# One table set for logarithm and exponential, shorter warm runs, and a head's mean square from two single-pass products in a two-layer encoder trunk

## The reference, cut to what matters

```python
def rmsnorm(x, g, eps=EPS):
    y = x * rsqrt(mean(x * x) + eps) * g
for layer in range(2):
    sh1, sc1, g1, sh2, sc2, g2 = split(silu(c) @ ada_w[layer] + ada_b[layer], 6)
    h = rmsnorm(x, norm_g[layer, 0]) * (1 + sc1) + sh1
    y = diff_attention(h) if layer == 0 else conformer_conv(h)
    x = x + g1 * y
    h = rmsnorm(x, norm_g[layer, 1]) * (1 + sc2) + sh2
    x = x + g2 * conv_ffn(h)
return rmsnorm(x, final_g)
# in diff_attention, per head: p = softmax(a) - lam * softmax(b); o = p @ v
#   o = rmsnorm(o, subln_g, 1e-5) * (1 - lambda_init), over the 128 values of a head
# in conformer_conv: silu(layernorm(causal_dwconv(glu(h @ w_pw1 + b_pw1), w_dw) + b_dw)) @ w_pw2 + b_pw2
```

## Time and profile before

| | |
|---|---|
| median of 3 runs (lowest to highest) | 1267.98 us (1267.55 to 1268.33) |
| the profiled execution: its time | 1265.96 us |
| the profiled execution: its span | 1264.2 us |
| mean granted clock of the matrix engine | 0.976 of full |
| busy share of the span: PE, DVE, ACT, POOL | 97%, 56%, 45%, 43% |
| chain that ended last, by engine | PE 81%, DVE 12%, issue 3%, ACT 2% |

### The profile page before, as it was taken

How to read it: one execution, slowest core, us unless ns; L and a number is a source line. 1 busy time by engine, 2 the same in 40 slices (tenths; PEclk the granted TensorE clock), 3 DMA queues, 4 the chain that set the end, 5 groups by cost and what they waited for, 6 DMA issues and landing times.

```text
span 1264.2 us, 16847 instructions
## 1 busy us (share of the span) xinstructions
PE 1231.0 (97%) x5494; PEld 983.4 (78%) x5494; DVE 702.3 (56%) x1157; ACT 567.5 (45%) x899; POOL 540.8 (43%) x273
## 2 busy tenths in 40 slices
PE   7999999989999999999999999999999999999996
PEld 7877777667888888888888776577888888888884
DVE  5667766753766733346887899972533333340002
ACT  4366656644543344442223666762544444442221
POOL 1333322223433444444442699744344444454440
PEclk6899999999999999999998999999999999999998
DMA  9744443222456422236763222113233232232321
GB/s 360 214 151 148 146 154 133 101 100 67 149 184 199 166 90 93 92 105 230 232 244 112 83 84 67 33 34 100 67 100 100 100 100 90 93 106 95 105 78 66
DMA packets 45639, 157.04 MB, mean 124 GB/s; under 512 B 5536, under 2 KB 5792, under 8 KB 45600
## 3 DMA queue, kind: packets, MB, share of 16 engines
q1 hardware_dynamic: 44928, 156.21, 37.0%
q10 hardware_dynamic: 672, 0.34, 0.1%
HBM read 154.10 MB, written 2.42 MB: 124 GB/s over the span
## 4 chain that ended last, share of the span: by engine, by line
PE 81%; DVE 12%; issue 3%; ACT 2%; POOL 1%; DMA 1%; DVEq 0%; SPq 0%; ACTq 0%; POOLq 0%
PE psum L917 24%; PE psum L918 24%; PE psum L919 24%; DVE psum L1754 6%; PE psum L947 2%; PE psum L928 1%; DVE psum L1480 1%; DVE pt_lo L1489 1%; PE psum L951 1%; PE psum L1074 1%; DVE acc L1331 1%; DMA ada_first<-ada_w 1%; POOL acc_p L515 1%; PE psum L1101 1%; PE psum L1113 0%
## 5 line engine op out<-in xcount | busy, mean ns | idle before, releaser
L502 POOL TENSOR_TENSOR w_lo<-w_raw,w_hi 128x1024 fp32r<-128x1024 f32 (+1 forms) x192 | 455.2, 2387 | 670.6 <-ACT w_hi L589 670.6
L917 PE MATMUL psum<-h_hi,w_hi 128*128 128x512 f32 x1152 | 465.9, 404 | 4.1 <-DVE x L1584 2.2
L918 PE MATMUL psum<-h_lo,w_hi 128*128 128x512 f32 x1152 | 452.5, 393 | 0.0
L919 PE MATMUL psum<-h_hi,w_lo 128*128 128x512 f32 x1152 | 452.1, 392 | 0.0
L917 PEld LDWEIGHTS psum<-h_hi,w_hi 128*128 128x128 f32 x1152 | 219.0, 190 | 54.3 <-issue 7.2
L919 PEld LDWEIGHTS psum<-h_hi,w_lo 128*128 128x128 f32 x1152 | 218.5, 190 | 46.9
L918 PEld LDWEIGHTS psum<-h_lo,w_hi 128*128 128x128 f32 x1152 | 218.7, 190 | 45.6 <-issue 3.4
L589 ACT ACTIVATE w_hi<-w_raw 128x1024 fp32r<-128x1024 f32 (+1 forms) x192 | 195.6, 1032 | 82.7 <-DMA w_raw<-w_tiles 82.6
L917 PE MATMUL psum<-a_hi,w_hi 128*128 128x512 f32 x352 | 137.1, 390 | 1.0 <-issue 1.0
L919 PE MATMUL psum<-a_hi,w_lo 128*128 128x512 f32 x352 | 137.0, 389 | 0.0
L918 PE MATMUL psum<-a_lo,w_hi 128*128 128x512 f32 x352 | 136.9, 389 | 0.0
(11 more groups left out here) (185 smaller groups left out, 1342.7 us busy)
## 6 DMA issues: line engine op xcount, KB each, us to landing
w_raw<-w_tiles SPq DMA_DIRECT2D x160, 512.0 KB, 3.4
ada_buf<-ada_w SPq DMA_DIRECT2D x32, 512.0 KB, 3.4
w_raw<-w_tiles SPq DMA_DIRECT2D x32, 448.0 KB, 3.2
ada_late<-ada_w SPq DMA_DIRECT2D x28, 512.0 KB, 5.2
ada_mid<-ada_w SPq DMA_DIRECT2D x20, 512.0 KB, 4.5
ada_first<-ada_w SPq DMA_DIRECT2D x16, 512.0 KB, 10.1
x<-x_in SPq DMA_DIRECT2D x4, 512.0 KB, 7.0
bias<-rel_scratch SPq DMA_DIRECT2D x8, 256.0 KB, 6.1
```

What stands on the lines that cost most here:

```text
L502: nc.gpsimd.tensor_tensor(w_lo[:, slot, 0:k], w_raw[:, (ph.tile + l) % 2, 0:k], f(w_hi[:, slot, 0:k]), ALU.subtract).then_inc(lo_done, 1)
L917: nc.tensor.matmul(dst, w_hi[:, slot, k], rhs_hi, start=first, stop=False)
L918: nc.tensor.matmul(dst, w_hi[:, slot, k], rhs_lo, start=False, stop=False)
L919: return nc.tensor.matmul(dst, w_lo[:, slot, k], rhs_hi, start=False, stop=last)
```

## The change

Five things change.

2. **A head's mean square.** ACT squares in place, in bank `OB`, and writes a rounded copy of the squares, `sq_hi`; DVE forms the rest, `sq_lo`, after its last piece of the conditioning and ahead of the bias of that (`ada_out`); PE multiplies both by ones of type fp32r, `ones_r`, which ACT makes once.
3. **Warm runs.** `keep_warm` has 12 repetitions instead of 18 ahead of UP0 and UP1, and 16 instead of 24 ahead of PW2.
4. **The seventh late chunk.** `last_ada(6)` moves from norm 2 to behind the layer norm's sums, ahead of `keep_warm(16)`; its sum lies in `acc_last`, its result in another bank.
5. **`late_out`** is called twice: for six chunks where it was, and for the seventh in the layer norm on DVE, behind the variance (L1778).

```diff
@@ -86,6 +86,7 @@
...
 PW1_FROM_2 = Phase(PW1.group + 2, PW1.tile + 4, 2, DK - 2)
+LN_EXP_SET = 6
 LATE0 = 4 + 8 * HEADS
@@ -165,6 +166,7 @@
...
         ones = sb("ones", [P, P])
+        ones_r = sb("ones_r", [P, P], F32R)
         big = cursor[0]
@@ -205,6 +207,8 @@
...
         o_sq = at("o_sq", [P, S], F32, offset_of["pad_v"])
+        sq_hi = at("sq_hi", [P, S], F32R, offset_of["pad_v"])
+        sq_lo = at("sq_lo", [P, S], F32R, offset_of["rms"])
@@ -229,7 +233,8 @@
...
         ada_late = at("ada_late", [P, 4, 2, S], F32, h_base)
-        acc_late = at("acc_late", [P, LATE, S], F32, h_base + 4 * 2 * S * 4)
+        acc_late = at("acc_late", [P, LATE - 1, S], F32, h_base + 4 * 2 * S * 4)
+        acc_last = at("acc_last", [P, S], F32, offset_of["pad_g"])
@@ -255,6 +260,7 @@
...
         DELTA_AT, RSTD_AT, SILU_AT = 4, 5, 6
+        LAST_OUT = 2
@@ -266,7 +272,7 @@
...
         rel_out, rel_back, store = sem("rel_out"), sem("rel_back"), sem("store")
-        ones_ready = sem("ones_ready")
+        ones_ready, ones_rounded = sem("ones_ready"), sem("ones_rounded")
         pool_mean = sem("pool_mean")
@@ -281,6 +287,7 @@
...
         pt_hi_done = sem("pt_hi_done")
+        sq_hi_done, sq_lo_done = sem("sq_hi_done"), sem("sq_lo_done")
         o_copied, o_squared, ms_read, o_inv = sem("o_copied"), sem("o_squared"), sem("ms_read"), sem("o_inv")
@@ -598,9 +605,18 @@
...
+            def load_ln_exp():
+
+                nc.scalar.add_instruction(mybir.InstLoadActFuncSet(
+                    name=nc.get_next_instruction_name(), engine=mybir.EngineType.Activation,
+                    act_func_set_id=LN_EXP_SET, ins=[], outs=[]))
+
             def load_table(function):
-                nc.scalar.activation(sm(TABLE), ones[:, 0:1], function)
+                if function == ACT.Ln:
+                    load_ln_exp()
+                else:
+                    nc.scalar.activation(sm(TABLE), ones[:, 0:1], function)
@@ -653,6 +669,9 @@
...
                 hi_of_h(0, m)
+
+            act.wait_ge(ones_ready, 1)
+            nc.scalar.activation(ones_r[:], ones[:], ACT.Copy).then_inc(ones_rounded, 1)
@@ -742,12 +761,13 @@
...
                 act.wait_ge(o_normed, lin(it, c + 1, 2))
-                nc.scalar.activation(o_sq[:], psum[:, OB], ACT.Square).then_inc(o_squared, 1)
+                nc.scalar.activation(psum[:, OB], psum[:, OB], ACT.Square).then_inc(o_squared, 1)
+                act.wait_ge(o_squared, lin(it, c + 1, 2))
+                nc.scalar.activation(sq_hi[:], psum[:, OB], ACT.Copy).then_inc(sq_hi_done, 1)
                 if next_qk:
...
                     o_high(m)
-                load_table(ACT.Ln)
                 act.wait_ge(ms_done, lin(it, c + 1, 2))
@@ -1059,6 +1079,8 @@
...
+            pe.wait_ge(ones_rounded, 1)
+
             def attention_steps(it, c):
@@ -1109,8 +1131,9 @@
...
                 def mean_square():
-                    pe.wait_ge(o_squared, lin(it, c + 1, 2))
-                    nc.tensor.matmul(psum[:, OB], ones[:], o_sq[:], start=True, stop=True).then_inc(ms_done, 1)
+                    pe.wait_ge(sq_lo_done, lin(it, c + 1, 2))
+                    nc.tensor.matmul(psum[:, OB], ones_r[:], sq_hi[:], start=True, stop=False)
+                    nc.tensor.matmul(psum[:, OB], ones_r[:], sq_lo[:], start=False, stop=True).then_inc(ms_done, 1)
@@ -1196,7 +1219,7 @@
...
             square_sum(1, 2)
-            keep_warm(18)
+            keep_warm(12)
@@ -1227,11 +1250,14 @@
...
                 pe.wait_ge(ada_used, 8 * (LATE_CH + q + 1))
-                ada_product(WARM, acc_late[:, q], at_=4 * q)
+                if q < LATE - 1:
+                    ada_product(WARM, acc_late[:, q], at_=4 * q)
+                else:
+                    ada_product(LAST_OUT, acc_last[:])
...
             square_sum(2, 1)
-            for q in range(1, LATE):
+            for q in range(1, LATE - 1):
                 last_ada(q)
@@ -1286,10 +1312,11 @@
...
                 dev_sums(n)
-            keep_warm(24)
+            last_ada(LATE - 1)
+            keep_warm(16)
             pairs(PW2, 4 * DK, x_done, 2 * DK, 2)
             square_sum(3, 2)
-            keep_warm(18)
+            keep_warm(12)
             pairs(UP1, 5 * DK, act_ready, FM, 1)
@@ -1400,7 +1427,7 @@
...
                     if m > lo:
-                        if n == 2 and m <= LATE:
+                        if n == 2 and m < LATE:
                             dve.wait_ge(ada_mm, LATE_CH + m)
@@ -1527,8 +1554,7 @@
...
-                def rest_of_ada():
-                    ada(3)
+                def ada_out():
                     dve.wait_ge(ada_mm, lin(it, CH0 + c + 1, 2))
@@ -1537,7 +1563,11 @@
...
                 if not lows:
-                    rest_of_ada()
+                    ada(3)
+                dve.wait_ge(sq_hi_done, lin(it, c + 1, 2))
+                V.tensor_tensor(sq_lo[:], psum[:, OB], f(sq_hi[:]), ALU.subtract).then_inc(sq_lo_done, 1)
+                if not lows:
+                    ada_out()
                 if next_qk:
@@ -1605,13 +1636,13 @@
...
-            def late_out():
-
-                dve.wait_ge(ada_mm, LATE_CH + LATE)
-                first, b = 4 * LATE_CH, PARAMS["ada_b"] + 4 * LATE_CH
-                V.tensor_tensor(mod[:, first:first + 4 * LATE], psum[:, WARM, 0:4 * LATE], prm[:, b:b + 4 * LATE],
+            def late_out(lo, hi, sums):
+
+                dve.wait_ge(ada_mm, LATE_CH + hi)
+                first, b = 4 * LATE_CH + 4 * lo, PARAMS["ada_b"] + 4 * LATE_CH + 4 * lo
+                V.tensor_tensor(mod[:, first:first + 4 * (hi - lo)], sums, prm[:, b:b + 4 * (hi - lo)],
                                 ALU.add).then_inc(sc_read, 1)
-                dve.wait_ge(sc_read, LATE0 + MID + 1)
+                dve.wait_ge(sc_read, LATE0 + MID + (1 if hi < LATE else 2))
@@ -1679,7 +1710,8 @@
...
                         k = 2 * (q % 4) + kk
-                        ada_part(ada_late[:, q % 4, kk], k, tile_of(acc_late, lin(i, c, 2)),
+                        total = acc_last[:] if isinstance(i, int) else tile_of(acc_late, lin(i, c, 2))
+                        ada_part(ada_late[:, q % 4, kk], k, total,
                                  lin(i, 8 * (LATE_CH + c) + k, 16))
@@ -1694,7 +1726,7 @@
...
             norm(2)
-            late_out()
+            late_out(0, LATE - 1, psum[:, WARM, 0:4 * (LATE - 1)])
             V.tensor_tensor(gated_bias[:], mod[:, GATE[2]:GATE[2] + DK],
@@ -1777,6 +1809,7 @@
...
                                    op0=ALU.mult, op1=ALU.subtract).then_inc(var_ready, 1)
+            late_out(LATE - 1, LATE, psum[:, LAST_OUT, 0:4])
             dve.wait_ge(delta_copied, 1)
```

## The result

| | before | after |
|---|---|---|
| median, first comparison | 1267.76 us (4 runs) | 1251.88 us (4 runs, 1246.89 to 1255.35) |
| ratio, 95% interval | | 0.9874 (0.9838 to 0.991) |
| second comparison | 1264.72 us (17 runs) | 1253.15 us (6 runs), 0.9908 (0.9883 to 0.9933) |
| third comparison | 1265.88 us (11 runs) | 1255.57 us (6 runs), 0.9909 (0.9881 to 0.9938) |
| profiled execution, its span | 1265.96 us, 1264.2 us | 1246.89 us, 1245.1 us |

The change is faster by 0.9 to 1.3%. The forecast, 1254.3 us, lies within 3 us of each of the three medians, and the range holds all of them. But the times spread: the first four of after over 0.7%, and the profiled one is the fastest of them.

What follows compares the result with a forecast made beforehand. PE, busy 1231 of 1264.2 us, was taken as the bound. The terms 2.8 + 3.3 - 0.7 + 3.9 + 1.7 + 1.4 + 1.3 = 13.7 us, off a median of 1267.98, gave 1254.3 us, range 1250.8 to 1259.2.

Steps and rivals of the forecast that it cites:

- Part 1: Heads 0 to 6: mean square as two fp32r products on PE saves 0.40 us a head, 2.8 us.
- the slower rival: Squares' rest late in every head behind DVE pieces stretched by POOL: 3.7 us wait a head, 1280 us; chance 0.03.
- Part 2: Start of head 7: fewer table loads give 1.3 us, DVE's unstretched conditioning piece 2.0 us; 3.3 us, ends 0 and 5.6.
- the stall of part 2 comes back: Rival: POOL and DVE collide again in head 7, costing 2.0 us, total 1256.3 us; chance 0.12.
- Part 3: Head 7's mean square: PE waits about 1.1 us, less 0.40 for the cheaper product; a loss of 0.7 us.
- Part 4: Norms 1 and 3: shorter warm run and earlier first rest let PE start 1.96 us earlier each, 3.9 us together.
- Part 5: Norm 2: moving out one conditioning product, priced at half speed, gains 1.7 us, ends 0.85 and 2.0.
- Part 6: Layer norm: DVE becomes the bound and the first rest comes earlier; 1.4 us gained, ends 0.7 and 2.0.
- the clock falls behind the shorter warm runs: Rival: PE starts at 1.2 GHz in the norms and layer norm, 1.6 us x 3, total 1259.1 us; chance 0.07.
- Part 7: Last norm: the uncovered table load goes from the chain, gaining 1.3 us.

Runs made afterwards that it cites:

- experiment 5: Changed kernel with `sq_hi` written twice in every head, so the squares' rounded part comes 0.63 us later: 1258.23 us, ratio 0.9941 to the kernel before.
- experiment 3: Changed kernel with the warm runs at 18, 24 and 18 repetitions again: 1258.24 us, ratio 0.9949 to the kernel before.
- experiment 8: Changed kernel with ACT's split of OUT's fourth tile moved later in head 7: 1248.07 us, ratio 0.9871 to the kernel before.
- experiment 2: Changed kernel with a head's mean square undone, one fp32 product as before: 1255.06 us, ratio 0.9929 to the kernel before.
- experiment 4: Changed kernel with the seventh late product of the conditioning back in norm 2: 1254.93 us, ratio 0.9916 to the kernel before.
- experiment 6: Kernel before with the table change alone: 1260.49 us, ratio 0.9973; also with the shorter warm runs alone: 1264.75 us, ratio 0.9994.

## Why the prediction was right, and where it was wrong

**Part 1, right, with less room than it had.** 0.39 to 0.41 us a head, predicted 0.40. The slack by the product's turn was 0.40 us by experiment 5, predicted 0.37, but the prediction left out that the load of the weights stands behind the same wait: only 0.10 us of lateness was free, and from there a late operand costs 0.27 us on top of the wait. So the slower rival's point of decision was nearer than it was put, 1.7 us of waiting and not 2.0. Its price was put too high: with `sq_lo` 0.7 behind 139.4, PE would wait some 2.6 us at 137.51 and not 3.7. No piece was stretched in the loop of the three profiles of after, where the gain of a head is the same to 0.07 us.

**Part 2 is the step that failed in the common case:** "by the same walk it starts some 0.2 us before POOL does, so I count the 2.0 us as gone". In the first profile DVE was ahead by 0.27 us and the 2.0 us were gone; DVE, POOL and PE there:

```profile
249.32 0.75 DVE L1358 SCALAR_TENSOR_TENSOR acc<-ada_buf,cact,acc 128x512 f32<-128x512 f32 x1
249.59 2.72 POOL L509 TENSOR_TENSOR w_lo<-w_raw,w_hi 128x1024 fp32r<-128x1024 f32 x1 [3.37 <-ACT w_hi L596]
252.81 0.55 PE L1114 MATMUL psum<-ident,z 128*128 128x128 f32 x3 [1.55 <-DVE z L1510]
```

In seven of the nine profiles that have the change, or most of it, and this order, the two more of after among them, PE waited 4.0 us again. The walk gave one outcome to a race that is decided by less than 0.3 us: DVE was ahead by 0.27 in the first profile and by 0.05 in experiment 3 (the two in which the wait is short), and POOL by 0.17 in the second. What tips it wasn't settled; the first profile had PE at 1.2 GHz for 6.8 us some 10 us ahead of the place and the second for 3.4, but experiment 3, where the wait is short, had 3.4 as well. The rival "the stall of part 2 comes back" was the common case, and 0.12 was far too little for it; its 1256.3 us is near the second and third comparison (0.9908 and 0.9909 of 1267.98 are 1256.3 and 1256.4 us). The loads' own part was right: with the stall, head 7's start gains 1.25 - 0.40 + 0.5 = 1.35 us, predicted 1.3. And the upper end, 5.6 us with the clock, is the state that experiment 8 makes permanent: 4.24 - 0.40 + 0.72 (the wait of 1.12 less 0.40) = 4.6 us.

**Part 3, right:** -0.5 by experiment 2, predicted -0.7; a wait of 1.11 us where 1.1 was predicted (1.43 in the first profile, where ACT's split of a tile held up the head's output).

**Part 4, right:** 1.81 to 1.88 us a norm, predicted 1.96; PE waits 0.3 us for the first rest, where none was forecast. That both cuts are needed was stated there and is shown: 0 with the tables alone, 0.57 with the runs alone.

**Part 5, mis-sized:** 2.5 us and not 1.7, beyond the upper end of 2.0. The product was priced at 1.2 GHz, 1.7 us, with the time at 1.2 GHz around it taken as fixed. It is worth 0.87 at 2.4 GHz, the lower end, and 1.6 more came since PE was at 1.2 GHz for 3.4 us and not for 6.8. That second part did not come in experiments 2 and 3.

**Part 6, right where the clock holds:** 1.01 to 1.07 us in four profiles, predicted 1.4. The first rest came 0.62 us earlier in the stage, as worked out (0.65). In the two profiles of after in which the clock fell for 6.8 us the stage lost 1.7 to 1.8, 2.8 us less; in experiment 4 it fell for 3.4 us and the stage lost 0.35. The rival "the clock falls behind the shorter warm runs" was right for this one place of its three: never at norms 1 and 3, where PE is idle for 0.3 us.

**Part 7, right:** 1.27 to 1.28 us. The 2.66 us of the Trainium skill (ScalarE: Activation LUTs, What ACT_TABLE_LOAD costs) would have made it 2.7; the runs show 1.28, the load's own duration, so nothing like a drain of 1.38 stood on this chain. The rule of the Trainium skill on the shared ports (SBUF — State Buffer, 🔬 SBUF: two separate sides), that the instruction that starts first holds them to its end, is borne out by experiment 8: the same instruction lasts 2.75 us when POOL began 0.17 before it and 0.75 when POOL came 1.5 behind.

**The sum.** 13.7 us was met by 15.9, 11.6 and 10.3 us of medians; without start and OUT, the three profiles of after gain 14.4, 9.9 and 8.4 us. So that the total came out near is in part luck. In the second profile the wait of 4 us took 1.8 us from the term of head 7, and the layer norm gave 3.1 less than its term, 2.8 of it by the clock. Against that the start gave 3.15 us, for which the prediction had nothing, and norm 2 0.8 more than its term. The prediction's own range was added up wrong as well: by the lower ends of parts 2, 5 and 6 it goes to 1259, not 1257. And of its signs two spoke against it in the second and third profile: a piece of DVE of over 2 us in head 7, and a fall of the clock behind the layer norm's warm run.

## What to carry to other kernels

A wait that came from two engines meeting at 0.2 us is not reliably removed by a change that moves one of them 0.4 us: put the one instruction clearly behind the other (here one ACT split moved behind five more of its instructions, which gave 4.8 us by the ratios 0.9871 and 0.9909) before you count the gain. Cut a warm run and the chain that it covers by the same amount: either alone gave 0 or 0.6 us of 1.9. Count the slack of an operand up to the load of weights that stands behind its wait, not up to the product. And take more than one profile of a kernel whose times spread: of the gain in the first one, 4.7 us lay at the start and in OUT, where the change does nothing.

## What the runs showed of the hardware

- Where PE's clock is at 1.2 GHz differs between executions of one program, at the start and in the layer norm above all. It fell late in or within 1 us behind each of ten waits of 4 us, and behind none of four waits of 1.6 to 2.0 us at the same place.
- After a wait for an operand, PE's first 128x512 product costs 0.50 us instead of 0.23 at 2.4 GHz, since its load of weights stands behind the wait (experiment 5).
- POOL's and DVE's collision goes both ways: where DVE's piece came first, by 0.27 us, POOL's rest lasted 2.72 us and not 2.38. And with both starting within 0.01 us of one another DVE's piece was the long one, 2.94 us (experiment 6).
- A stage whose instructions are the same as the changed kernel's can take 1.6 us more by the clock (norm 2 in experiment 3), so its gain in one profile is not its price.
